# Strassen's seven products for the gated feed-forward projections of the second block

## The chip, the cores and the metric

The kernel runs on one core of one Trainium2 chip. The metric is the device time in microseconds (us). Before the change the median of three runs is 2394.31 us (2393.95 to 2394.52). A difference of under 0.2% (some 5 us) can hardly be told from none.

## The reference, cut to what matters

The program takes 512 tokens of width 1024 through two blocks of two layers each, in float32. The change touches the feed-forward part of the second block's two layers, which the reference computes as

```python
D_FF_2 = 2816
def swiglu(h, w_gate, w_up, w_down):
    return (jax.nn.silu(h @ w_gate) * (h @ w_up)) @ w_down
x = x + rmsnorm(swiglu(rmsnorm(x, ffn_pre_g[layer]), ...), ffn_post_g[layer])
```

with `w_gate` and `w_up` of 1024 x 2816 and `w_down` of 2816 x 1024. The first block has an ungated part of this kind: relu(h w_up) squared, times w_down.

## The kernel before, in words

**Three passes.** Values are kept with features on the 128 partitions and the 512 tokens in the free dimension. Every float32 operand is split into a high and a low fp32r part, and a product is three matmuls: high by high, high by low, low by high. The weights are split on the chip. SyncE loads a slot (a 512 x 512 or smaller piece of a weight matrix) into one of three raw buffers (`load_slots`, L317; a load waits until the low parts of the slot three before it are made), ScalarE copies it to the high part (`stream_hi` L341, `rows_hi` L329), GpSimd subtracts to get the low part (`stream_lo`, L397, operations on L414), and TensorE takes one 128 x 512 tile after the other as its low part is counted (`group_tiles`, matmuls on L452). Slots go through ScalarE and GpSimd strictly in the order in which they were planned.

**A group** is one filling of half of PSUM (four banks of 128 x 512). A direct projection group has 8 tiles of rows, 4 banks and 3 passes: 96 matmuls over 512 columns. A half of a down projection has 4 tiles of rows and 48 such matmuls. Groups alternate between the halves of PSUM, and a bank is taken again when VectorE has emptied it (`bank_free`).

**Strassen's seven products** are used before the change in the first block's feed-forward part (`quarter_tiles`, L488, matmuls on L485). The group's product is cut in two slots, each of seven units; a unit is one product of quarters: 4 tiles x 3 passes = 12 matmuls over 256 columns, so a group has 168. Four of a slot's seven weight units are sums of quarters of the raw weights, made by VectorE (`units_sum`, L380, operations on L395); the others are taken as loaded. ScalarE then makes the high part (`units_hi`, L377) and GpSimd the low one (L409). The low part is written over the sum, so GpSimd must wait for those later sums that still read it:

```python
pool.wait_ge(sems["sum_done"], slot.sum0 + (2, 4, 3, 4)[SUMS.index(k)])
```

with `SUMS = (1, 2, 3, 5)`. Unit 2 thus waits for all four sums. The weight units lie in eight cells used in turn; a cell comes free when TensorE has used its unit. Before TensorE's units 4, 5 and 6 the products of earlier units must be taken out of PSUM: a copy by ScalarE (`p1_copied`), then two adds (`p5_added`) and one more (`p7_added`) by VectorE (`middle`, L1936, rows on L1942 to L1946). For the moving side, four sums of quarters of h are made once per layer: ScalarE writes h in full precision (`hf`, L1704), VectorE subtracts (`t_total`, L1927), ScalarE makes the high parts (`t_high`, L1701) and VectorE the low ones.

**The second block's feed-forward part** before the change is direct. `plan_second` (L1212) plans 11 projection groups, each with 256 gate and 256 up features (2816 = 11 x 256), and the down projection in halves: first a short one for the first group's 256 rows, then four full ones of 512 rows and a last one that is joined to the norms (`Boundary`). Around them TensorE does projection groups 0 and 1, the short down projection, group 2, then down projection, group, group, and so on. `gated` (L2325, L2560) is the work after a group: VectorE takes four banks out with the norm's factor (L969, L978), ScalarE applies silu, VectorE multiplies (L2576), and the result is split (`hid_hi` L2333 by ScalarE, `hid_lo` L2579 by VectorE). `down` (L2582) adds a down projection's banks into `acc` (L2590). ScalarE's and VectorE's queues are written out by hand in `second_layer` (L2025): an instruction that waits holds up all behind it.

## Time and profile before

| | |
|---|---|
| runs | 2394.31 us median of 3 (2393.95 to 2394.52) |
| profiled execution | 2391.58 us, of which span 2389.8 us |
| TensorE busy | 2341.5 us (98%), 12840 matmuls |
| VectorE busy | 1347.5 us (56%) |
| ScalarE busy | 1047.3 us (44%) |
| GpSimd busy | 1229.2 us (51%) |
| DMA | 214.58 MB, mean 90 GB/s |

PE, DVE, ACT, POOL and SP are TensorE, VectorE, ScalarE, GpSimd and SyncE. In a timeline a row is a start, a duration, then the engine, line and operation; "x4" merges four in a row, and a bracket names the idle time before it and what ended it. The feed-forward parts of the second block run from about 1472 to 1812 us and from about 2008 to 2352 us of the span.

### The profile page before, as it was taken

The page shows a single profiled execution, that of the slowest core. Times are in us where ns is not written, and L with a number is a line of the kernel's source. Part 1 is how long each engine was busy: PE and PEld are TensorE (multiplying, and loading weights), DVE is VectorE, ACT ScalarE, POOL GpSimd, SP SyncE. Part 2 cuts the span into 40 slices and gives each one's busy share as a digit, 9 for nine tenths or more (in the row PEclk, how much of TensorE's full clock was granted, in tenths as well). Part 3 has the DMA queues.
Part 4 walks back from the last instruction along what each step waited for, and adds up shares of the span by engine and source line. Part 5 has one row for each costly group of instructions (what it writes and reads, how often), then busy time and mean ns, then how long its engine had stood idle before and what let it go on. Part 6 is the DMA issues. An engine that isn't in the chain of part 4 may idle for free.

```text
span 2389.8 us, 32547 instructions
## 1 busy us (share of the span) xinstructions
PE 2341.5 (98%) x12840; PEld 1929.5 (81%) x12840; DVE 1347.5 (56%) x2210; ACT 1047.3 (44%) x1654; POOL 1229.2 (51%) x915
## 2 busy tenths in 40 slices
PE   8999999999999999999999999999999999999997
PEld 6777688989877767898988769888889779888887
DVE  4687587675548866867665446322225768322224
ACT  5345573444343456553444455322224485322223
POOL 4435277786543253787783453554454334554442
PEclk9999999999999999999999999999999999999999
DMA  5213123232322131233232212322332312322331
GB/s 187 75 62 107 36 88 106 91 105 89 106 89 71 56 113 54 88 107 106 89 123 88 85 36 62 115 88 88 106 106 89 106 53 80 115 89 88 105 106 36
DMA packets 153975, 214.58 MB, mean 90 GB/s; under 512 B 7776, under 2 KB 94944, under 8 KB 153568
## 3 DMA queue, kind: packets, MB, share of 16 engines
q1 hardware_dynamic: 153824, 212.51, 27.3%
q8 instruction: 102, 1.67, 0.3%
q14 instruction: 49, 0.40, 0.1%
HBM read 208.30 MB, written 2.10 MB: 88 GB/s over the span
## 4 chain that ended last, share of the span: by engine, by line
PE 86%; DVE 5%; ACT 4%; POOL 3%; issue 2%; SPq 0%; DMA 0%; ACTq 0%; DVEq 0%; POOLq 0%
PE ps L452 64%; PE ps L485 13%; POOL w_lo L414 2%; PE ps L1024 2%; PE ps L1005 2%; PE ps L1047 1%; PE ps L2185 1%; PE ps L1499 1%; DVE h_lo L748 1%; DVE x L871 1%; DVE tmp_both L866 1%; PE ps L1537 1%; ACT w_hi L353 0%; PE ps L1546 0%; ACT L672 0%
## 5 line engine op out<-in xcount | busy, mean ns | idle before, releaser
L414 POOL TENSOR_TENSOR w_lo<-raw,w_hi 128x512 fp32r<-128x512 f32 (+1 forms) x648 | 859.6, 1365 | 982.4 <-ACT w_hi L353 977.1
L452 PE MATMUL ps<-h_hi,w_hi 128*128 128x512 f32 (+1 forms) x1248 | 507.4, 407 | 10.5 <-POOL w_lo L414 10.4
L452 PE MATMUL ps<-h_hi,w_lo 128*128 128x512 f32 (+1 forms) x1248 | 487.4, 391 | 0.0
L452 PE MATMUL ps<-h_lo,w_hi 128*128 128x512 f32 (+1 forms) x1248 | 487.2, 390 | 0.0
L452 PE MATMUL ps<-hid_hi,w_hi 128*128 128x512 f32 x928 | 366.9, 395 | 10.3 <-POOL w_lo L414 4.8
L452 PE MATMUL ps<-hid_hi,w_lo 128*128 128x512 f32 x928 | 361.5, 390 | 0.0
L452 PE MATMUL ps<-hid_lo,w_hi 128*128 128x512 f32 x928 | 361.4, 389 | 0.0
L353 ACT ACTIVATE w_hi<-raw 128x2048 fp32r<-128x2048 f32 (+2 forms) x145 | 246.3, 1724 | 172.9 <-PE ps L452 110.8
L452 PEld LDWEIGHTS ps<-h_hi,w_hi 128*128 128x128 f32 (+1 forms) x1248 | 234.5, 188 | 72.4 <-issue 18.0
L452 PEld LDWEIGHTS ps<-h_hi,w_lo 128*128 128x128 f32 (+1 forms) x1248 | 233.8, 187 | 51.5 <-issue 0.2
L452 PEld LDWEIGHTS ps<-h_lo,w_hi 128*128 128x128 f32 (+1 forms) x1248 | 234.3, 188 | 50.7 <-issue 5.5
L409 POOL TENSOR_TENSOR c_lo_more<-c_f_more,c_hi_more 128x512 fp32r<-128x512 f32 x112 | 171.7, 1548 | 120.7 <-DVE c_f_more L395 112.6
L452 PEld LDWEIGHTS ps<-hid_hi,w_hi 128*128 128x128 f32 x928 | 174.4, 188 | 52.9 <-POOL w_lo L414 8.3
L452 PEld LDWEIGHTS ps<-hid_hi,w_lo 128*128 128x128 f32 x928 | 174.2, 188 | 36.7
L452 PEld LDWEIGHTS ps<-hid_lo,w_hi 128*128 128x128 f32 x928 | 174.3, 188 | 35.1 <-issue 1.0
L377 ACT ACTIVATE c_hi_more<-c_f_more 128x512 fp32r<-128x512 f32 x112 | 70.5, 631 | 240.5 <-DVE c_f_more L395 238.9
L969 DVE TENSOR_TENSOR tmp_both<-ps,rstd 128x512 f32<-128x512 f32 x48 | 33.0, 690 | 248.2 <-PE ps L452 248.1
L2330 ACT ACTIVATE tmp_both<-tmp_both 128x512 f32<-128x512 f32 x44 | 27.6, 631 | 267.7 <-DVE tmp_both L969 266.4
L1865 DVE TENSOR_TENSOR x<-x,ps 128x512 f32<-128x512 f32 x160 | 102.3, 679 | 75.3 <-PE ps L452 75.3
L1130 ACT ACTIVATE p<-p,stat 128x128 f32<-128x128 f32 (+3 forms) x128 | 71.8, 561 | 136.8 <-DVE stat L1092 136.6
L485 PE MATMUL ps<-t_hi,c_lo_more 128*128 128x256 f32 x448 | 126.5, 282 | 0.0
L485 PE MATMUL ps<-t_lo,c_hi_more 128*128 128x256 f32 x448 | 126.3, 282 | 0.0
(355 smaller groups left out, 4524.6 us busy)
## 6 DMA issues: line engine op xcount, KB each, us to landing
raw<-in_w_down SPq DMA_DIRECT2D x32, 1024.0 KB, 4.9
raw_u<-in_w_up SPq DMA_DIRECT2D x28, 1024.0 KB, 5.2
raw<-in_ffn_w_gate SPq DMA_DIRECT2D x44, 512.0 KB, 3.8
raw<-in_ffn_w_up SPq DMA_DIRECT2D x44, 512.0 KB, 4.7
raw<-in_w_in SPq DMA_DIRECT2D x20, 1024.0 KB, 5.0
raw<-in_ffn_w_down SPq DMA_DIRECT2D x20, 1024.0 KB, 4.9
raw<-in_w_out SPq DMA_DIRECT2D x8, 1024.0 KB, 6.4
raw<-in_ev_w_in SPq DMA_DIRECT2D x8, 1024.0 KB, 5.1
```

The costliest lines, as they stand in the source:

```text
L353: act.activation(w_hi[slot.buf][:, k:k + n, 0:slot.width], raw[r][:, k:k + n, 0:slot.width], ACT.Copy).then_inc(sems["hi_split"], n)
L377: act.activation(unit(slot.hi(i)), of, ACT.Copy).then_inc(sems["hi_split"], 1)
L409: pool.tensor_tensor(unit(slot.lo(k)), of, unit(slot.hi(k)).bitcast(F32), ALU.subtract).then_inc(sems["lo_split"], 1)
L414: pool.tensor_tensor(slot.lo(k)[:, 0:slot.width], raw[r][:, k, 0:slot.width], slot.hi(k)[:, 0:slot.width].bitcast(F32), ALU.subtract).then ...
L452: mm = pe.matmul(o, lh, rh, start=first and q == 0, stop=last and q == 2, skip_group_check=True)
L485: mm = pe.matmul(o, lh, rh, start=first and q == 0, stop=last and q == 2, skip_group_check=True)
L969: sg["bank_free"].by(dve.tensor_tensor(o, src, rstd[:, 0:width], ALU.mult))
L1005: mm = pe.matmul(ps[:, e, 0:n], a_q[rows, j, q], a_k[rows, kb, 0:n], start=c == 0, stop=last)
L1024: mm = pe.transpose(ps[:, 2, kb * P:(kb + 1) * P], p_t[i % self.PB][:, kb * P:(kb + 1) * P], ident)
L1130: sg["p_ready"].by(act.activation(p_t[i % self.PB][:, 0:w], p_t[i % self.PB][:, 0:w], ACT.Exp, bias=sn[:, i:i + 1], scale=SCALE, accum_out ...
L1865: sg["bank_free"].by(dve.tensor_tensor(x[:, b, :], x[:, b, :], ps[:, HALF * st.groups[g].half + m, :], ALU.add))
L2330: sg["relu_ready"].by(act.activation(tmp[m][:], tmp[m][:], ACT.Silu))
```

## The change

Of the 11 projection groups of each second-block layer, nine (numbers 2 to 10) are computed by seven products; each slot then holds 128 gate and 128 up columns side by side, loaded by two transfers. Seven cells take the place of eight here: a unit always gets the cell of the same unit of the slot before. The order on TensorE is now group 0, group 1, the two halves of the short down projection, group 2, group 3, and then one half of a down projection ahead of each of the groups 4 to 10, the last half, and the joined one. ScalarE makes `hf` and VectorE `t_total` ahead of `gated` for group 0. VectorE's order in one group is `strassen`; the banks of the down half that TensorE did before the group are added behind the group's first joins, ahead of the last two weight sums. The diff, cut:

```diff
@@ -188,6 +188,16 @@
...
+        ffn_cells = [("gap", 0), ("more", 0), ("more", 1), ("more", 7), ("tab", 0), ("h", 0), ("h", 1)]
@@ -293,10 +303,11 @@
...
+                    self.need[s % RING] += 16 * len(src)
...
+                    pieces = [(w.rearrange("(k p) c -> p k c", p=P), 256 // len(src) * n, 256 // len(src))
+                              for n, w in enumerate(src)]
+                    slot = Slot(pieces, UNITS, self.need[s % RING], None, self.rows)
@@ -1235,19 +1248,24 @@
...
+            def gated_quarters(c0, half):
+                return st.quarters([[w[:, c0 + P * i:c0 + P * i + P] for w in (wg, wu)] for i in range(2)], half)
+
+            def down(r0, rows, n, half):
+                return st.group(cols(wd, [(512 * n, 512)], r0), [rows], half)
 
             pl.s_ffn = len(st.slots)
-            pl.up, pl.down = [up(CH2 * 512, first)], []
-            for c in range(CH2):
-                if 0 < c < CH2 - 1:
-                    pl.down.append(down(512 * (c - 1), KT, 1 - first))
-                pl.up.append(up(512 * c, 1 - first))
-                if c == 0:
-                    pl.down.append(down(CH2 * 512, REST2 // P, first))
-                pl.up.append(up(512 * c + 256, first))
-            pl.down.append(down(512 * (CH2 - 2), KT, 1 - first))
+            pl.up, pl.down = [up(CH2 * 512, first), up(0, 1 - first)], []
+            pl.down.append([down(CH2 * 512, REST2 // P, n, (first + n) % 2) for n in range(2)])
+            pl.up.append(gated_quarters(256, first))
+            pl.up.append(gated_quarters(512, 1 - first))
+            for n in range(4, UPS):
+                c, e = divmod(n - 4, 2)
+                if e == 0:
+                    pl.down.append([])
+                pl.down[-1].append(down(512 * c, KT, e, first))
+                pl.up.append(gated_quarters(256 * (n - 1), 1 - first))
+            pl.down[-1].append(down(512 * (CH2 - 2), KT, 1, first))
@@ -1300,11 +1318,23 @@
...
+                turn, downs = 0, 0
+                for i in range(pl.s_ffn, pl.s_out + 2):
+                    slot, n = st.slots[i], i - pl.s_ffn
+                    if slot.quarters:
+                        slot.cells = [ffn_cells[(turn + k) % len(ffn_cells)] for k in range(slot.rows)]
+                        turn += slot.rows
+                        slot.buf = None
+                    elif n < 4:
+                        slot.buf = (4, 3, turns[0], turns[1])[n]
+                    elif n < 6:
+                        slot.cells, slot.buf = [(turns[0], 2 * (n - 4) + k) for k in range(2)], None
+                    elif i >= pl.s_out:
+                        slot.buf = 2 + i - pl.s_out
+                    else:
+                        slot.buf = turns[1 - downs % 2]
@@ -2195,19 +2237,21 @@
...
+                for e in range(2):
+                    rest(tiles_of(pl.down[0][e], FEAT, hid_hi, hid_lo, ready=("hid_lo_done", lo0)))
+                quarter_tiles(pe, pl.up[2], 0, "t_done", t_hi2, t_lo2)
+                quarter_tiles(pe, pl.up[3], 2, None, t_hi2, t_lo2)
+
+                def down(c, e):
+                    pe.wait_ge(*at("hid_lo_done", 4 * c + 6))
+                    rest(tiles_of(pl.down[1 + c][e], FEAT, hid_hi, hid_lo, k0=KT * (1 - c % 2)))
+
+                for n in range(4, UPS):
+                    down(*divmod(n - 4, 2))
+                    quarter_tiles(pe, pl.up[n], 2 * (n - 2), None, t_hi2, t_lo2)
+                down(CH2 - 2, 1)
+                pe.wait_ge(*at("hid_lo_done", 2 * UPS))
+                to_next.tensor(pe, 2, None, KT)
@@ -2332,14 +2376,55 @@
...
+                for k in range(DB):
+                    sg["hf_done"].by(act.activation(hf[k // 4][:, k % 4, :], x[:, k, :], ACT.Copy, scale=pl.pre_ffn.gain(k)))
+                gated(pl.up[0], 0)
+                for n in range(4):
+                    t_high(n)
+                stream_hi(act, s_ffn + 6)
+                units_hi(act, u_slot(2), 0, 5)
+                gated(pl.up[1], KT)
+                units_hi(act, u_slot(2), 5, 7)
+                for n in range(2, UPS):
+                    nx = u_slot(n + 1) if n + 1 < UPS else None
+                    ub = u_slot(n) + 1
+                    units_hi(act, ub, 0, 1)
+                    p1_copy(n, 0)
+                    units_hi(act, ub, 1, 7)
+                    if n >= 3:
+                        stream_hi(act, ub + 2)
+                    p1_copy(n, 1)
+                    if nx is not None:
+                        units_hi(act, nx, 0, 5)
+                    silu(n, 0)
+                    if nx is not None:
+                        units_hi(act, nx, 5, 6)
+                    silu(n, 1)
+                    if nx is not None:
+                        units_hi(act, nx, 6, 7)
+                    hid_high(n, 1)
+                    hid_high(n, 0)
+                stream_hi(act, s_out + 2)
                 if even:
@@ -2589,17 +2674,87 @@
...
+                def join(n, i):
+                    t, u = slice(256 * i, 256 * i + 256), 2 * (n - 2) + i
+                    dve.wait_ge(*at("p1_copied", u + 1))
+                    dve.wait_ge(sems["unit_used"], st.slots[u_slot(n) + i].unit0 + 3)
+                    link(dve, dve.tensor_tensor(u_p16[:, i, :], u_p1[:, i, :], bank(n, 3)[:, t], ALU.add))
+                    sg["p5_added"].by(dve.tensor_tensor(u_q[0][:, i, :], u_p16[:, i, :], bank(n, 1)[:, t], ALU.add))
+                    dve.wait_ge(*at("p5_added", u + 1))
+
+                def join_more(n, i):
+                    t = slice(256 * i, 256 * i + 256)
+                    dve.wait_ge(sems["unit_used"], st.slots[u_slot(n) + i].unit0 + 4)
+                    sg["p7_added"].by(dve.tensor_tensor(u_q[0][:, i, :], u_q[0][:, i, :], bank(n, 2)[:, t], ALU.add))
+
+                def strassen(n):
+                    ub, nx = u_slot(n) + 1, u_slot(n + 1) if n + 1 < UPS else None
+                    units_sum(dve, ub, 0, 1)
+                    join(n, 0)
+                    units_sum(dve, ub, 1, 2)
+                    join_more(n, 0)
+                    if n >= 4:
+                        down(1 + (n - 4) // 2, n % 2)
+                    units_sum(dve, ub, 2, 4)
+                    join(n, 1)
+                    if nx is not None:
+                        units_sum(dve, nx, 0, 1)
+                    join_more(n, 1)
+                    dve.wait_ge(*at("p7_added", 2 * (n - 1)))
+                    link(dve, dve.tensor_tensor(u_q[0], u_q[0], both(rstd, 1), ALU.mult))
+                    if nx is not None:
+                        units_sum(dve, nx, 1, 2)
+                    dve.wait_ge(sems["unit_used"], st.slots[ub].unit0 + 5)
+                    ins = dve.tensor_tensor(u_q[1], two(bank(n, 0)), both(rstd, 0), ALU.mult)
+                    sg["bank_free"].by(ins)
+                    if nx is not None:
+                        units_sum(dve, nx, 2, 3)
+                    dve.wait_ge(sems["unit_used"], st.slots[ub].unit0 + 6)
+                    sg["bank_free"].by(dve.tensor_tensor(u_q[2], u_p16, two(bank(n, 1)), ALU.add))
+                    dve.wait_ge(sems["bank_free"], BANKS + HALF * pl.up[n] + 2)
+                    sg["gate_ready"].by(dve.tensor_tensor(u_q[2], u_q[2], both(rstd, 1), ALU.mult))
+                    if nx is not None:
+                        units_sum(dve, nx, 3, 4)
+                    dve.wait_ge(sems["bank_ready"], HALF * (pl.up[n] + 1))
+                    sg["bank_free"].by(dve.tensor_tensor(u_q[3], u_p16, two(bank(n, 2)), ALU.add), 2)
+                    dve.wait_ge(sems["bank_free"], BANKS + HALF * pl.up[n] + 4)
+                    link(dve, dve.tensor_tensor(u_q[3], u_q[3], both(rstd, 0), ALU.mult))
+                    dve.wait_ge(*at("relu_ready", 2 * n + 2))
+                    sg["v_ready"].by(dve.tensor_tensor(u_q[2], u_q[2], u_q[0], ALU.mult))
+                    sg["v_ready"].by(dve.tensor_tensor(u_q[3], u_q[3], u_q[1], ALU.mult))
+                    for e in (1, 0):
+                        dve.wait_ge(*at("hid_hi_done", 2 * n + 2 - e))
+                        sg["hid_lo_done"].by(dve.tensor_tensor(hid_quad(hid_lo, n, e), u_q[3 - e],
+                                                               hid_quad(hid_hi, n, e).bitcast(F32), ALU.subtract))
+
+                dve.wait_ge(*at("hf_done", DB))
+                for n in range(4):
+                    t_total(n)
+                gated(pl.up[0], 0)
+                for n in range(4):
+                    t_low(n)
+                units_sum(dve, u_slot(2), 0, 3)
+                gated(pl.up[1], KT)
+                units_sum(dve, u_slot(2), 3, 4)
+                down(0, 0)
+                down(0, 1)
+                for n in range(2, UPS):
+                    strassen(n)
+                down(CH2 - 1, 1)
                 to_next.vector(dve)
```

## Rows read from the trace of the kernel before

**Rows 1.** TensorE's busy time and granted clock, the page's parts 1 and 2:

```profile
PE 2341.5 (98%) x12840; PEld 1929.5 (81%) x12840; DVE 1347.5 (56%) x2210; ACT 1047.3 (44%) x1654; POOL 1229.2 (51%) x915
...
PEclk9999999999999999999999999999999999999999
```

**Rows 2.** The chain of waits, the page's part 4, shares by engine:

```profile
PE 86%; DVE 5%; ACT 4%; POOL 3%; issue 2%; SPq 0%; DMA 0%; ACTq 0%; DVEq 0%; POOLq 0%
```

**Rows 3.** Windows: stretch, its length, each engine's busy time, clock, DMA share, GB/s:

```profile
414.50:434.50 20.00, 20.00 (x169) 19.99 (x168) 9.30 (x15) 10.85 (x20) 13.06 (x11) 1.00 0.21 71
434.50:456.30 21.80, 21.80 (x98) 18.05 (x97) 19.89 (x18) 7.17 (x13) 19.50 (x12) 1.00 0.39 129
1554.40:1576.20 21.80, 21.80 (x98) 18.06 (x97) 8.07 (x12) 8.56 (x6) 17.10 (x14) 1.00 0.34 102
```

**Rows 4.** TensorE's timeline: the run's start, then first matmuls of groups:

```profile
8.78 0.63 PE L452 MATMUL ps<-h_hi,w_lo 128*128 128x512 f32 x1
...
10.92 0.49 PE L452 MATMUL ps<-h_lo,w_hi 128*128 128x512 f32 x1
...
414.50 0.29 PE L485 MATMUL ps<-h_hi,c_hi_more 128*128 128x256 f32 x1
...
434.52 0.40 PE L452 MATMUL ps<-hid_hi,w_hi 128*128 128x512 f32 x1
...
456.30 0.29 PE L485 MATMUL ps<-h_hi,c_hi_more 128*128 128x256 f32 x1
...
1521.16 0.39 PE L452 MATMUL ps<-hid_hi,w_hi 128*128 128x512 f32 x1
```

**Rows 5.** TensorE's timeline, the first block's first down projection:

```profile
349.94 0.50 PE L452 MATMUL ps<-hid_hi,w_hi 128*128 128x512 f32 x1 [0.71 <-POOL w_lo L414]
...
352.88 0.50 PE L452 MATMUL ps<-hid_hi,w_hi 128*128 128x512 f32 x1 [0.73 <-POOL w_lo L414]
```

**Rows 6.** VectorE's timeline in the first block's Strassen stage:

```profile
443.47 3.48 DVE L1971 TENSOR_TENSOR hid_lo<-tmp_both,hid_hi 128x512 fp32r<-128x512 f32 x2
...
450.27 4.26 DVE L1865 TENSOR_TENSOR x<-x,ps 128x512 f32<-128x512 f32 x7
...
458.02 0.69 DVE L395 TENSOR_TENSOR c_f_more<-raw_u 128x512 f32<-128x512 f32 x1 [0.83 <-PE ps L485]
...
462.00 0.41 DVE L1942 TENSOR_TENSOR rs<-p_more,ps 128x256 f32<-128x256 f32 x1
...
463.71 0.69 DVE L395 TENSOR_TENSOR c_f_more<-raw_u,c_f_more 128x512 f32<-128x512 f32 x1 [0.40 <-PE ps L485]
```

**Rows 7.** GpSimd's timeline in the same stage:

```profile
442.95 5.15 POOL L409 TENSOR_TENSOR c_lo_more<-c_f_more,c_hi_more 128x512 fp32r<-128x512 f32 x3
...
451.47 2.53 POOL L409 TENSOR_TENSOR c_lo_more<-raw_u,c_hi_more 128x512 fp32r<-128x512 f32 x2
...
464.55 2.54 POOL L409 TENSOR_TENSOR c_lo_more<-c_f_more,c_hi_more 128x512 fp32r<-128x512 f32 x2 [3.02 <-DVE c_f_more L395]
...
470.78 10.62 POOL L414 TENSOR_TENSOR w_lo<-raw,w_hi 128x512 fp32r<-128x512 f32 x7
```

**Rows 8.** VectorE's timeline, start of the first block's Strassen stage:

```profile
312.80 1.23 DVE L1927 TENSOR_TENSOR t_sum<-hf 128x1024 f32<-128x1024 f32 x1 [2.44 <-ACT hf L1704]
```

**Rows 9.** ScalarE's timeline, the same start:

```profile
307.76 5.00 ACT L1704 ACTIVATE hf<-x,vec 128x512 f32<-128x512 f32 x8
...
321.00 1.06 ACT L1701 ACTIVATE t_hi<-t_sum 128x1024 fp32r<-128x1024 f32 x1 [1.18 <-DVE t_sum L1927]
```

**Rows 10.** VectorE's timeline, start of the second block's feed-forward part:

```profile
1506.65 0.69 DVE L978 TENSOR_TENSOR tmp_both<-ps,rstd 128x512 f32<-128x512 f32 x1 [11.38 <-ACT rstd L693]
...
1510.69 1.30 DVE L2579 TENSOR_TENSOR hid_lo<-sq_both,hid_hi 128x512 fp32r<-128x512 f32 x2
```

**Rows 11.** ScalarE's timeline, the same start:

```profile
1510.03 1.24 ACT L2333 ACTIVATE hid_hi<-sq_both 128x512 fp32r<-128x512 f32 x2 [0.30 <-DVE sq_both L2576]
```

**Rows 12.** Issues of Strassen slots: KB each, us to landing:

```profile
raw_u<-in_w_up SPq DMA_DIRECT2D x28, 1024.0 KB, 5.2
```

More of the change, by code:

```diff
@@ L1194, in plan_first @@
                 if c < CH1:
[L1195 removed]
+                    pl.up.append(st.quarters([[a["w_up"][L][:, 512 * c + 256 * i:512 * c + 256 * i + 256]] for i in range(2)], half))
                     half = 1 - half
@@ L2602, in _, with t_total, t_low @@
-                down(CH2 - 1)
+                def t_total(n):
+                    b11, b12, b21, b22 = (hf[i][:, :, tokens(e)] for i in range(2) for e in range(2))
+                    p, q = ((b12, b11), (b22, t_sum2[:, 0]), (b22, b12), (b21, t_sum2[:, 1]))[n]
+                    if n in (1, 3):
+                        dve.wait_ge(*at("t_summed", (n + 1) // 2))
+                    sg["t_summed"].by(dve.tensor_tensor(t_sum2[:, n], p, q, ALU.subtract))
+                def t_low(n):
+                    dve.wait_ge(*at("t_high", n + 1))
+                    sg["t_done"].by(dve.tensor_tensor(t_lo2[:, n], t_sum2[:, n], t_hi2[:, n].bitcast(F32), ALU.subtract))
@@ new lines, in bank @@
+                def bank(n, b):
+                    return ps[:, HALF * st.groups[pl.up[n]].half + b, :]
+                def join(n, i):
[5 more added lines that the diff above has]
+                    dve.wait_ge(*at("p5_added", u + 1))
```

93 lines of the change are left out of this document (45 added, 48 removed).

## The prediction

> **What bounds the kernel now.** I read the page first: TensorE is busy 98% of the span at full granted clock [rows 1], and the chain of waits is 86% TensorE's [rows 2]. Then the windows: in the second block's stage TensorE is busy all of a 21.8 us stretch, while VectorE has 8.07 and GpSimd 17.10 us of work at its fullest (the last of [rows 3]). So time falls only if TensorE's work falls and the helpers keep up. Last, the timelines of the first block, which already does there what the change brings here: they give a price for almost every new step.
>
> **TensorE's part.** A Strassen group lasts from 414.50 to 434.52, 20.02 us; the 96 matmuls over 512 columns behind it last to 456.30, 21.78 us [rows 4]. A direct group has the same 96. So a changed group saves 1.76 us, and nine in each of two layers 31.7 us. That is all there is to win.
>
> Here the row is weighed against a rule. Over 256 columns a matmul takes 20.02/168 = 119 ns, over 512 columns 21.78/96 = 227 ns: more than half. The Trainium skill ("TensorE: Matmul & The Clock Gate", section Back-to-back issue gap) gives N/2.4 + 2.5 ns for an isolated gap, which as an estimate is 109 and 216 ns, 2.4 us a group and 43 us in all; the same section warns that it counts no weight loads. The trace disagrees.
>
> **What the helpers pay.** Alone, a GpSimd low part of 128x512 takes 2.54/2 = 1.27 us, say 1.26 with the 2.53 row; a VectorE operation on PSUM 4.26/7 = 0.61. But a VectorE operation with two SBUF inputs next to a GpSimd one slows both: VectorE 3.48/2 = 1.74, GpSimd 5.15/3 = 1.72 [rows 6, 7]. So each such operation pushes GpSimd back by 1.72 - 1.26 = 0.46 us. PSUM adds do not (the seven run at 0.61 while GpSimd works). The Trainium skill ("SBUF — State Buffer", Who interferes with whom) calls it an exclusive lock for the full instruction; that would be 1.26 + 0.61 = 1.87 a pair, and 0.8 us more stall per down half than below, 12 us in all. The row's 1.72 decides.
>
> **The steady cycle**, a Strassen group and half a down projection, seven times a layer. Clock t from TensorE's first matmul; a unit is 20.02/14 = 1.43 us; a wait on a unit ends 0.29 late (the sum at 458.02 for the unit done at 457.73) [rows 6]. VectorE has one more wait here than in the first block, since with seven cells slot 1's unit k must wait for slot 0's unit k, not k-1.
> - First join: third unit, 4.29 + 0.29, then two of 0.45: 5.5. Weight sum 0.65: 6.1. Third add 0.45: 6.6.
> - Four adds of the down half at 0.61: 9.0. Before, they lay beside idle time; here the last two weight sums stand behind them.
> - Two weight sums: 10.3. In the first block the last sum starts at 463.71 - 456.30 = 7.4, and GpSimd goes on at 464.55, 8.25 [rows 6, 7]. Here at 10.4, because unit 2 waits for all four sums.
> - GpSimd then has five units and the four tiles of the next down half, 9 x 1.26 = 11.3. Beside them VectorE asks for five two-input operations (first sum of the next slot, the up factor, second and third sum, the gate factor): 2.3. Last tile ready at 24.0.
> - TensorE wants that tile at 20.02 + 3 x 0.68 = 22.06. It stalls 1.95 us. The first block shows this form: tile after tile of its first down projection waits for GpSimd, 0.71 and 0.73 us [rows 5]; in its steady stage GpSimd starts those tiles at 470.78, t = 14.5 [rows 7], and none waits.
> So the cycle is 20.02 + 10.89 + 1.95 = 32.86 us, against 21.78 + 10.89 = 32.67 now. The gain of 1.76 is spent and 0.2 more. VectorE's tail (two products, two low parts, all beside GpSimd) ends about 0.5 us before it is needed for the next group. The banks are free at t = 25, long before TensorE is back at 33.
>
> **The start of a layer.** Now evacuation of group 0 starts at 1506.65, and its high and low parts end at 1511.27 and 1511.99 [rows 10, 11]. New ahead of it: ScalarE's eight `hf`, 5.0 us, and VectorE's four `t_total` at some 1.2, 4.75 us [rows 8, 9]. Both ends move by 9.75, to 1521.0 and 1521.7; TensorE asks at 1521.16 [rows 4], so the hidden values are just in time. The short down projection's weights are not: ScalarE splits them behind group 0's high parts and four `t_high` of 1.0 (1.06 [rows 9]): 1524.9, first tile 0.5, GpSimd 1.26: 1526.7. Stall 5.5 us.
> - Group 2: VectorE takes group 1 through `gated` (5.3, as group 0 now [rows 10]), the fourth weight sum, eight bank copies (4.9) and a sum before its first join, done about 1545.9; TensorE needs it 7.15 us after 1537.6. It is 1.1 late and the third add 0.3 more. Stall 1.4.
> - Group 3 follows group 2 with no down projection between. VectorE's fourth sum for it ends some 3.8 us after the group begins (0.9 if nothing met GpSimd, 7 if all did; I went through both queues). Then six two-input operations at 1.72, since GpSimd has five units to do as well, and the join 0.9: 15.0. TensorE needs it at 7.15. Stall 7.9.
> - The first full down half stalls 1.1, the other seven 1.95. At the end the joined projection's weights are split behind the last group's: 0.5.
>
> **At nothing:** the transfers. They are two of 512 KB for one of 1 MB; one of 1 MB lands in 5.2 us [rows 12], and every slot has 9 us or more from its raw buffer's release to its first use. ScalarE has idle time: 10.85 us of work in a 20 us group [rows 3]. The longest stall, near 8 us, might cost TensorE's pace: at the run's start matmuls come 0.43 us apart instead of 0.23 for 3.1 us [rows 4]. Between 0 and 1.5 us each; I take 0.
>
> **Sum.** A layer: 5.5 + 1.4 + 7.9 + 1.1 + 7 x 1.95 + 0.5 = 30.0 of stalls, less 15.8 gained: +14.2. Two layers: +28.4. The profiled execution took 2391.58 (span 2389.8 and 1.8 around it), so 2420.0; the runs' median lies 2.7 above it: 2422.7, I say 2422.
>
> **Rivals.**
> 1. *The helpers keep pace, faster.* Place: the unit 2 low part at t = 10.4. If it starts by 8.45, the down half's tiles are ready and the steady stall is nil. For it: the first block gets to 8.25. Against it: four adds and the seventh cell lie before it. Startup would then cost some 11 a layer: 2394.3 - 31.7 + 22 = 2385; with that hidden too, 2363.
> 2. *It comes out even.* Steady stalls nil, the start as priced (15.3 a layer): 2394.3 - 31.7 + 30.6 = 2393.
> 3. *VectorE becomes the bound.* If all 15 two-input operations of a cycle meet GpSimd, VectorE has 25.8 + 7.2 (adds and joins on PSUM) = 33.0 us, more than the cycle, and each first join is late as in group 3. For it: in the first block's down stretch VectorE is busy 19.89 of 21.80 us [rows 3]. Against: GpSimd is idle from about t = 4 to 10. From 1.5 us a cycle: 2422 + 14 x 1.5 = 2443.
> 4. *The place of the adds does nothing.* Behind the last sums they would free GpSimd at 9.5 (unit 5's cell is free only at 8.9). The stall would still be about 1: this moves 14 us, not the sign.
>
> **How the numbers follow.** Forecast 0.60 (its own range 2406 to 2438), rival 3 0.12, rival 2 0.10, rival 1 0.18. The range takes in the upper half of rival 1 and most of rival 3: 2382 to 2442. Under 0.2% (4.8 us) a measurement of this kernel can't tell from no change. Faster: rival 1 and a third of rival 2, 0.21; same: 0.08; slower: 0.71.
>
> **What would show it.** Strassen groups of the second block at 20.0 us where nothing waits; waits of L452's `hid` matmuls on GpSimd's low parts of 1 to 2 us in each down half; a gap of 5 to 6 us ahead of the short down projection; in group 3 a gap of 5 us or more that VectorE's join ends; GpSimd idle in each group until t = 10, ended by a VectorE weight sum; GpSimd's mean low part above 1.4 us. I am wrong if TensorE's idle time per layer in this stage is under 16 us, above all if the down halves run through.

## The result, and the profile after

The changed kernel takes 2418.99 us (median of 4 runs, 2416.49 to 2424.13), the kernel before 2394.13 us beside it (4 runs, 2392.93 to 2394.52): ratio 1.0107, 95% interval 1.0089 to 1.0125, slower. The profiled execution is the run of 2416.49 us, with a span of 2414.7 against 2389.8. It is the fastest of the four; every stretch below is read from the one profiled execution of its kernel, every time and ratio from all runs.

The page's parts 1 and 4 of the changed kernel:

```profile
PE 2329.3 (96%) x14136; PEld 1969.8 (82%) x14136; DVE 1685.6 (70%) x2514; ACT 1152.8 (48%) x1934; POOL 1449.0 (60%) x1023
...
PE 68%; DVE 12%; POOL 10%; ACT 5%; issue 4%; SPq 0%; DMA 0%; DVEq 0%; ACTq 0%; POOLq 0%
```

TensorE is busy 12 us less than in [rows 1] (matmuls at half pace, told of below, count as busy) and the chain leaves it for VectorE and GpSimd, 22% together where [rows 2] has 8. The windows give the first full steady cycle in three parts, a Strassen group, a down half and the next group (busy time of PE, PEld, DVE, ACT and POOL, then clock, DMA share and GB/s):

```profile
1601.40:1621.40 20.00, 20.00 (x169) 20.00 (x168) 13.92 (x19) 7.58 (x12) 15.17 (x12) 1.00 0.29 85
1621.40:1633.80 12.40, 11.58 (x51) 8.93 (x51) 12.30 (x12) 5.25 (x9) 12.40 (x8) 1.00 0.36 120
1633.80:1653.80 20.00, 20.00 (x169) 20.00 (x168) 13.92 (x19) 7.58 (x12) 15.17 (x12) 1.00 0.29 86
```

The group runs without a gap; the down half lasts 12.3 us instead of 10.9, and VectorE and GpSimd are busy throughout. Below, layer 0 and layer 1 are the two layers of the second block. The gaps in TensorE's work, its timeline in layer 0 from the last matmul of the direct groups on (in brackets the idle time and what ended it):

```profile
1521.31 0.39 PE L464 MATMUL ps<-h_hi,w_lo 128*128 128x512 f32 x1
1528.13 0.77 PE L464 MATMUL ps<-hid_hi,w_hi 128*128 128x512 f32 x1 [6.43 <-issue]
1528.70 0.63 PE L464 MATMUL ps<-hid_lo,w_hi 128*128 128x512 f32 x1
...
1533.79 0.39 PE L464 MATMUL ps<-hid_lo,w_hi 128*128 128x512 f32 x1
...
1566.08 0.39 PE L497 MATMUL ps<-t_hi,c_hi_more 128*128 128x256 f32 x1 [1.21 <-POOL c_lo_more L421]
...
1571.56 0.36 PE L497 MATMUL ps<-h_hi,c_hi_tab 128*128 128x256 f32 x1 [2.09 <-ACT p_more L2385]
...
1575.93 0.36 PE L497 MATMUL ps<-h_hi 128*128 128x256 f32 x1 [2.72 <-DVE tmp_both L2696]
...
1657.20 0.50 PE L464 MATMUL ps<-hid_hi,w_hi 128*128 128x512 f32 x1 [0.72 <-POOL w_lo L426]
```

The first pair is the gap ahead of the short down projection, 6.6 us beyond the usual spacing; behind it matmuls start 0.43 us apart for 5.3 us before they are back at 0.23. The next three lie in group 3, which follows group 2 with nothing between. The last is the fourth low part of a down half, and its like stands in every cycle. What ended the first gap, which TensorE's row calls "issue", ScalarE's and GpSimd's timelines show:

```profile
1524.99 2.17 ACT L349 ACTIVATE w_hi<-raw 128x512 fp32r<-128x512 f32 x4
```

```profile
1525.68 7.44 POOL L426 TENSOR_TENSOR w_lo<-raw,w_hi 128x512 fp32r<-128x512 f32 x4 [16.43 <-ACT w_hi L349]
```

GpSimd stood idle until ScalarE rounded the short down projection's weights.

**Where the time went, by stretch.** All matmuls of a direct group and a down half cost 21.78 and 10.89 us; a changed group measures 20.07. In layer 0, from the direct groups' end to the first full down half (1521.54 to 1588.92) are 67.4 us, of which 10.88 + 2 x 20.07 = 51.0 are work: **16.4 us of stall at the start** (16.5 in layer 1). The eight down halves last 12.46, six between 12.28 and 12.36, and 11.53: **10.8 us of stall in the halves**. From layer 0's joined projection to the next layer's work (its first matmul on L677) are 31.14 us against 29.65 before: 1.5 at the **boundary** between the two layers. Nine groups give back 9 x 1.71 = 15.4. From the end of the direct groups to the joined projection a layer is 305.8 us against 294.3, 11.5 more in either layer (16.4 + 10.8 - 15.4 = 11.8; the kernel before had some 0.3 of waits in this stretch too); twice that, 1.5 and 0.4 ahead of it are the 24.9 us of the two spans.

### The profile page after: what moved, and what is told of

Read it like the earlier page. It is cut to its first block, busy times and chain, and to the rows that moved or that the text cites. A ratio compares the mean times of both kernels' runs of the same rounds, so it can differ in the third digit from the quotient of the medians.

```text
span 2414.7 us, 36406 instructions
## 1 busy us (share of the span) xinstructions
PE 2329.3 (96%) x14136; PEld 1969.8 (82%) x14136; DVE 1685.6 (70%) x2514; ACT 1152.8 (48%) x1934; POOL 1449.0 (60%) x1023
## 4 chain that ended last, share of the span: by engine, by line
PE 68%; DVE 12%; POOL 10%; ACT 5%; issue 4%; SPq 0%; DMA 0%; DVEq 0%; ACTq 0%; POOLq 0%
PE ps L464 43%; PE ps L497 15%; POOL w_lo L426 5%; DVE c_f_more L407 2%; PE ps L1036 2%; PE ps L1017 2%; DVE acc L2675 1%; PE ps L1059 1%; POOL c_lo_more L421 1%; POOL h_lo L421 1%; POOL c_lo_tab L421 1%; POOL h_hi L421 1%; PE ps L2227 1%; PE ps L1533 1%; DVE h_lo L760 1%
## 5 line engine op out<-in xcount | busy, mean ns | idle before, releaser
L426 POOL TENSOR_TENSOR w_lo<-raw,w_hi 128x512 fp32r<-128x512 f32 (+2 forms) x504 | 712.7, 1447 | 699.4 <-ACT w_hi L365 661.2
L421 POOL TENSOR_TENSOR c_lo_more<-c_f_more,c_hi_more 128x512 fp32r<-128x512 f32 x220 | 329.3, 1513 | 216.5 <-DVE c_f_more L407 153.2
L464 PE MATMUL ps<-hid_hi,w_hi 128*128 128x512 f32 x928 | 373.1, 402 | 35.0 <-POOL w_lo L426 15.4
L464 PE MATMUL ps<-h_hi,w_hi 128*128 128x512 f32 (+1 forms) x672 | 283.3, 422 | 11.1 <-POOL w_lo L426 11.1
L464 PE MATMUL ps<-h_hi,w_lo 128*128 128x512 f32 (+1 forms) x672 | 263.3, 392 | 0.0
L464 PE MATMUL ps<-h_lo,w_hi 128*128 128x512 f32 (+1 forms) x672 | 263.1, 391 | 0.0
L497 PE MATMUL ps<-t_hi,c_hi_more 128*128 128x256 f32 x880 | 248.3, 282 | 2.4 <-POOL c_lo_more L421 2.4
L407 DVE TENSOR_TENSOR c_f_more<-raw_u 128x512 f32<-128x512 f32 x128 | 170.4, 1331 | 41.7 <-PE ps L497 41.2
L497 PEld LDWEIGHTS ps<-t_hi,c_hi_more 128*128 128x128 f32 x880 | 165.8, 188 | 3.3 <-POOL c_lo_more L421 3.3
L497 PEld LDWEIGHTS ps<-t_lo,c_hi_more 128*128 128x128 f32 x880 | 165.9, 188 | 0.0
L497 PEld LDWEIGHTS ps<-t_hi,c_lo_more 128*128 128x128 f32 x880 | 165.6, 188 | 0.0
```

The source lines that it names most:

```text
L407: sg["sum_done"].by(dve.tensor_tensor(o, p, q, op))
L421: pool.tensor_tensor(unit(slot.lo(k)), of, unit(slot.hi(k)).bitcast(F32), ALU.subtract).then_inc(sems["lo_split"], 1)
L426: pool.tensor_tensor(slot.lo(k)[:, 0:slot.width], raw[r][:, k, 0:slot.width], slot.hi(k)[:, 0:slot.width].bitcast(F32), ALU.subtract).then ...
L464: mm = pe.matmul(o, lh, rh, start=first and q == 0, stop=last and q == 2, skip_group_check=True)
L497: mm = pe.matmul(o, lh, rh, start=first and q == 0, stop=last and q == 2, skip_group_check=True)
```

## The experiments

All change the changed kernel and leave its arithmetic alone; only orders and places move. My theory was the prediction's: low parts come late because of where steps stand in the engines' queues. Its rival was that VectorE and GpSimd lack time as such. The expectations of all twelve stand in full, those that failed too. Ratios are to the kernel before. Executions differ by some us ahead of the stage (the short down projection was asked for between 1521.5 and 1526.3), so stretches are compared by their own length.

### e1: the adds behind the last sums

```
                     units_sum(dve, ub, 1, 2)
                     join_more(n, 0)
-                    if n >= 4:
-                        down(1 + (n - 4) // 2, n % 2)
                     units_sum(dve, ub, 2, 4)
+                    if n >= 4:
+                        down(1 + (n - 4) // 2, n % 2)
```

> The changed kernel with VectorE's four down adds behind the second weight slot's last two sums instead of ahead of them. If the stall of 1.44 us in a down half comes from GpSimd waiting for these sums until 10.25 us after the group's start: GpSimd goes on some 0.9 us earlier, in each of the 14 halves with adds the stall falls by 0.8 to 1.0, 2405 to 2409 us. If the place of the adds does not matter (the rival in which the stall is GpSimd's amount of work or the shared time of its operations with VectorE's): within 2 us of 2419.

2413.22 us, ratio 1.0072 (1.0054 to 1.0090). That is outside the expected 2405 to 2409. A steady down half lasts 11.7 to 11.75, a stall of 0.8 instead of 1.44: GpSimd goes on 9.64 us after the group's start instead of 10.25, and now the fourth sum itself waits 0.66 us for TensorE to free its cell. The last half has no stall, the first none in layer 0 and 1.6 as before in layer 1. So the halves give 5.8 and 4.1 us. The starts take 16.9 and 15.8 instead of 16.4 and 16.5, and the boundary, reached earlier, 36.0 instead of 31.1: 9.9 + 0.1 - 4.9 = 5.1, and 5.8 came of it in the time. So the place of the adds counts, and something at the boundary takes half of it back. GpSimd's row for unit 2 in the group that begins at 1635.39, then VectorE's and GpSimd's timelines at the boundary, show both:

```profile
1645.03 2.55 POOL L421 TENSOR_TENSOR c_lo_more<-c_f_more,c_hi_more 128x512 fp32r<-128x512 f32 x2 [2.04 <-DVE h_f L407]
```

```profile
1836.20 5.08 DVE L656 TENSOR_TENSOR ssum<-ssum,sq_both 128x512 f32<-128x512 f32 x1
```

```profile
1825.64 15.10 POOL L426 TENSOR_TENSOR w_lo<-raw,w_hi 128x512 fp32r<-128x512 f32 x12
```

One sum of squares took 5.08 us. It ends 0.5 us after GpSimd's run of low parts (1840.74), which was at its undisturbed pace (15.10/12 = 1.26). More of this below.

### e2, e5, e8: the start's queues

e2 moves `stream_hi(act, s_ffn + 6)`, the short down projection's weights, ahead of ScalarE's `gated(pl.up[0], 0)`.

> ScalarE rounds the short down projection's weights right behind its eight copies of the normed block, ahead of the first gated columns. If ScalarE's queue makes the 6.6 us gap at the layer's start: the gap falls below 1.5 us, the 2.8 us of slow pace behind it go with it, and groups two and three give some of it back because their weights' parts are made no earlier: 4 to 9 us less per layer, 2401 to 2411. If the gap is the wait for the hidden values or for the transfers: within 2 us of 2419, with the gap ending on another releaser.

2421.56 us, ratio 1.0113 (1.0098 to 1.0128): nothing gained. TensorE's timeline in layer 0 has two gaps in place of one:

```profile
1527.27 0.50 PE L464 MATMUL ps<-hid_hi,w_hi 128*128 128x512 f32 x1 [2.92 <-DVE hid_lo L2664]
1536.52 0.77 PE L464 MATMUL ps<-hid_hi,w_hi 128*128 128x512 f32 x1 [3.53 <-DVE tmp_both L981]
```

The first ends on the hidden values, the second on the bank that VectorE empties when it comes to group 1. ScalarE's queue was the last releaser of the gap, not its only cause. In layer 1 the second gap is shorter and the start takes 14.8 us instead of 16.5; the boundary, 35.9 us instead of 31.1, spends that and more. e5 put VectorE in order too, and moved ScalarE's `hf` and `t_high` behind the columns they had stood ahead of. VectorE's part:

```
-                dve.wait_ge(*at("hf_done", DB))
-                for n in range(4):
-                    t_total(n)
                 gated(pl.up[0], 0)
+                dve.wait_ge(*at("hf_done", DB))
                 for n in range(4):
-                    t_low(n)
-                units_sum(dve, u_slot(2), 0, 3)
+                    t_total(n)
                 gated(pl.up[1], KT)
-                units_sum(dve, u_slot(2), 3, 4)
+                for n in range(4):
+                    t_low(n)
+                units_sum(dve, u_slot(2), 0, 4)
```

> Both engines take the first gated columns ahead of everything for the Strassen groups: ScalarE gated columns, short down's weights, the eight block copies, second gated columns, four roundings; VectorE gated columns, four block differences, second gated columns, four low parts, four weight sums. With ScalarE's order alone mended (the run before) the 6.8 us gap only split into 3.3 us for the hidden values and 3.9 us for the bank that VectorE empties late. If the gap is both engines' order: no gap ahead of or in the short down projection and no slow pace, 9.4 us per layer gained, of which group two's wait for its low parts takes 2 to 5 back: 2404 to 2412. If it is VectorE's total of work up to group three: the gaps move into groups two and three whole, within 3 us of 2419.

2420.43 us, ratio 1.0114 (1.0097 to 1.0131). The gap ahead of the short down projection is gone, and stands at full size ahead of group 2:

```profile
1539.18 0.55 PE L497 MATMUL ps<-h_hi,c_hi_gap 128*128 128x256 f32 x1 [6.31 <-DVE acc L2672]
```

e8 filled 6 us of VectorE's and ScalarE's idle time ahead of group 1's columns with three weight sums and four roundings, and emptied each bank when it was wanted, the short projection's second half behind group 2's first joins. VectorE's part, as it differs from e5:

```
                 gated(pl.up[0], 0)
+                units_sum(dve, u_slot(2), 0, 3)
...
                 gated(pl.up[1], KT)
+                down(0, 0)
                 for n in range(4):
                     t_low(n)
-                units_sum(dve, u_slot(2), 0, 4)
-                down(0, 0)
-                down(0, 1)
+                units_sum(dve, u_slot(2), 3, 4)
```

> The mended order of the start, and with it work put where the engines stood idle: VectorE's first three weight sums and ScalarE's first four roundings of group two go into the 6 us ahead of the second gated columns, VectorE empties the short down projection's first half ahead of the four low parts, its second half behind group two's first joins. The last start run turned the gap into one of 6.7 us ahead of group two that ended on VectorE's copy out of the bank: if it is that queue, it goes, and groups two and three keep their 6 to 7 us: 9 to 10 us per layer below the changed kernel, 2399 to 2405. If the amount of VectorE's work decides, 2412 or more.

2418.91 us, ratio 1.0097 (1.0077 to 1.0118): no gain. But here the gaps did shrink, in layer 0 from 13.1 to 9.8 us, 4.0 in group 2 and the rest in group 3. In layer 0 TensorE's pace took it back, and the start stalls 17.3 us; in layer 1 the start takes 14.8 instead of 16.5, and the boundary 35.9 instead of 31.1. Two windows of e8, behind the first gap and among the last ones:

```profile
1540.80:1550.00 9.20, 9.20 (x54) 9.20 (x55) 6.02 (x10) 1.57 (x4) 7.86 (x6) 0.66 0.34 100
...
1570.00:1580.00 10.00, 7.65 (x35) 7.41 (x36) 8.19 (x9) 3.45 (x7) 6.04 (x5) 0.55 0.36 105
```

The granted clock is 0.66 and 0.55 where the changed kernel, with much the same three gaps in group 3, has 1.00 in layer 0 and 0.83 in layer 1, where the clock fell behind the second gap:

```profile
1570.00:1580.00 10.00, 5.72 (x46) 5.58 (x47) 9.04 (x9) 4.08 (x8) 6.50 (x5) 1.00 0.37 107
...
2119.00:2129.00 10.00, 6.55 (x42) 6.31 (x43) 9.45 (x10) 3.67 (x7) 6.50 (x5) 0.83 0.36 106
```

Beside the gaps e8 loses 7.5 of its 17.3 us in layer 0, some 6 of them to matmuls at half pace, the changed kernel 3.3 of its 16.4, and 4.5 of its 16.5 in layer 1 with the same orders. So the pace is not set by the orders alone. TensorE's row of the first, and GpSimd's of e9, which has the same start:

```profile
1540.81 0.58 PE L497 MATMUL ps<-t_hi,c_hi_more 128*128 128x256 f32 x1 [3.97 <-POOL c_lo_more L421]
```

```profile
1543.04 2.83 POOL L435 TENSOR_TENSOR c_lo_more<-c_f_more,c_hi_more 128x512 fp32r<-128x512 f32 x2 [15.01 <-DVE h_f L421]
```

GpSimd stood idle for 15 us. Unit 2's low part overwrites the second sum, which the fourth still reads, and I had left the fourth behind the low parts of the block sums: my own order, not the amount of work.

### e3, e4: slots ahead, and a down half between

e3 takes each full down half's weights one group earlier through SyncE's loads, ScalarE's rounding and GpSimd's low parts, TensorE's order unchanged:

```
+            for n in range(3, UPS):
+                c, e = divmod(n - 3, 2)
+                s = st.slot_ahead(cols(wd, [(512 * e, 512)], 512 * c), KT, 1)
+                pl.up.append(gated_quarters(256 * (n - 1), 1 - first))
...
+                pl.down[-1].append(st.group_of(s, first))
```

> Each full down half's weights are loaded, rounded and split one Strassen group earlier, ahead of that group's own weights; TensorE's order is as it was. If the down half waits for low parts that are just late in GpSimd's order: the 1.44 us go in all 14 steady halves and the 1.57 of the first, about 21 us, and group three starts with four tiles more ahead of it, up to 5 us per layer lost: 2398 to 2409. If GpSimd is short of time as such, each group's first tiles wait instead and the time is within 3 us of 2419.

2406.79 us, ratio 1.0049 (1.0034 to 1.0064). Two windows of the trace, a group and its down half:

```profile
1606.40:1626.40 20.00, 20.00 (x169) 20.00 (x168) 14.51 (x19) 7.59 (x12) 14.48 (x12) 1.00 0.29 86
1626.40:1637.30 10.90, 10.90 (x50) 9.04 (x49) 10.80 (x11) 4.82 (x9) 10.90 (x7) 1.00 0.40 134
```

No down half waits: cycles of 30.98 us against 32.67 before. So in the steady stage the rival falls: the helpers do a cycle's work in less than TensorE needs. The rest of the sum: halves -21.2, start 19.9 and 19.1 instead of 16.4 and 16.5 (four more low parts ahead of group 3, a gap of 4.2 us there), boundary 34.3 instead of 31.1: -21.2 + 6.1 + 3.2 = -11.9, measured -12.2.

e4 ran the short down projection's second half between groups 2 and 3.

> The second half of the short down projection runs between Strassen groups two and three instead of ahead of group two. If group three's 7.0 us of stall are the join of group two and group three's weights with nothing between them: up to 5.4 us of other matmuls lie there now, group two starts 5.4 us earlier and waits part of that for its own weights; 2 to 5 us less per layer, 2409 to 2415. If it is GpSimd's and VectorE's total of work at the start: within 2 us of 2419.

2419.42 us, ratio 1.0104 (1.0089 to 1.0119), as the rival had it; start 16.8 and 15.5. In layer 0 group 3 stalled 5.6 instead of 7.0 and group 2, begun earlier, 2.7 instead of nothing. The stall moved once more; in layer 1 it lost 1.0 on the way.

### e6, e7, e9, e10: combinations

e6 joins e5's start and e3's earlier slots, all but the first down half's; e7 adds ScalarE's `p1_copy(n + 1, 0)` ahead of `hid_high(n, ...)` for group 3.

> The order of the run above, and every down half's weights but the first one group earlier. If the two losses are apart: another 1.44 us in each of 14 halves, less 2 to 3 us that VectorE's block sums at the end of each layer take back (as where all halves were ahead): 14 to 16 below the run above, 2389 to 2397. If a third place binds instead, 2400 or more.

> As the run above, and in ScalarE's order the copy of each Strassen group's first product stands ahead of the rounding of the group before's hidden values. If the 2.37 us wait in group three is that copy's place: 0 to 2.4 us less per layer (the join of VectorE comes 3 us later and may bind anyway), 0 to 5 us below the run above. If only VectorE's join binds: no change within 1 us.

2413.61 and 2412.88 us, ratios 1.0090 (1.0075 to 1.0105) and 1.0084 (1.0069 to 1.0099). e6 is far above the 2389 to 2397 that was expected; e7 is 0.7 below e6, which is what was expected if only VectorE's join binds. All but the first half run through, and the start takes 21.9 and 22.6 us in e6, 21.1 and 23.1 in e7. ScalarE rounds two down slots in one go in group 3, and the copy that the join needs waits behind the second's transfer (a gap of 4.8 us in e6, ended by the join). e7's copy changed the releaser of group 3's wait and not its end.

e9 is e8's start, e6's slots with that second slot behind the copy, e7's copy, and group 2's `hid_low` behind group 3's first joins. e10 adds e4's split.

> The start of the run above; every down half's weights but the first one group earlier, with the second such slot's rounding behind the copy of group three's second first product (it delayed that copy by 5.1 us before); and for group two alone the hidden values' low parts behind group three's first joins, with ScalarE's copy ahead of its two roundings. If all of these are queue order: 14 halves times 1.44 less 5 at the layers' ends, and 3 to 5 us of group three's wait per layer: 22 us or so below the run above, 2377 to 2387, under the kernel before. If GpSimd and VectorE lack time as such: 2390 or more.

> As the run above, with the short down projection's second half between groups two and three. Group three's join gets 5.4 us, group two starts 5.4 us earlier, when its low parts are made only some 4 us later: between 3 us per layer better and 3 us worse than the run above, 2374 to 2390; if group three's wait is gone and group two waits instead by as much, the two runs are even.

2407.15 and 2411.81 us, ratios 1.0059 (1.0040 to 1.0077) and 1.0073 (1.0058 to 1.0089); start 19.5 and 21.1 in e9, 21.7 and 22.0 in e10. Both missed by 20 us and more, e9 on the side of its rival; e10 is 4.7 us slower than e9, where 6 either way was expected. In e9 the waits are GpSimd's 15 idle us again and, in group 3, VectorE's timeline:

```profile
1592.28 1.32 DVE L421 TENSOR_TENSOR c_f_more<-raw_u 128x512 f32<-128x512 f32 x1 [7.12 <-DMA raw_u<-in_ffn_w_up]
1593.52 0.41 DVE L2726 TENSOR_TENSOR tmp_both<-tmp_both,ps 128x256 f32<-128x256 f32 x1
```

A weight sum for group 4 waits 7.12 us for its transfer, which could start only once GpSimd had left the raw buffer, three slots back; the third add of group 3 (L2726) is queued behind it, and TensorE behind that.

### e11 and e12: the fourth sum, and no double run

e11 is e9 with VectorE's `units_sum(dve, u_slot(2), 3, 4)` moved ahead of `gated(pl.up[1], KT)`, one more of ScalarE's roundings ahead of group 1's columns and the last two between its `t_high`, and group 3's `join_more(n, 1)` ahead of the sum that waited.

> The orders of e9 with two places mended that its trace showed. VectorE's fourth weight sum of group two, for which GpSimd's low part of the second stood still 15 us, goes ahead of the second gated columns (ScalarE's roundings five to seven with it); and in group three the sum for the next group, which waited 7 us for its transfer with the last join behind it, goes behind that join. If the start is order after all: of the 19.5 us of stall per layer between the first gated columns and the first full down projection, 4 in group two and 5 to 6 in group three go: 2384 to 2392, at or under the kernel before. If what is left is bound by the work of VectorE and GpSimd or by the seven cells that group three's parts share with group two: less than 4 us per layer goes, 2400 or more.

2406.15 us, ratio 1.0047 (1.0033 to 1.0060). Up to the first full down half the stall is 10.8 us (11.0 in layer 1), the least of all runs; then group 4 takes 27.6 instead of 20.1 (29.0 in layer 1). VectorE's and GpSimd's timelines:

```profile
1588.60 6.52 DVE L421 TENSOR_TENSOR c_f_more<-raw_u 128x512 f32<-128x512 f32 x1 [6.56 <-DMA raw_u<-in_ffn_w_up]
```

```profile
1583.29 10.03 POOL L440 TENSOR_TENSOR w_lo<-raw,w_hi 128x512 fp32r<-128x512 f32 x8
```

An operation that takes 0.69 us alone took 6.52, until GpSimd was through its run of eight (1593.32) and one more low part (1594.57); in layer 1 its like took 6.69. e12 keeps the start, drops the double run by having all halves ahead as in e3, and leaves out e11's last move.

> The start of e11 and group three's order, with all down halves' weights one group earlier as in e3, so that GpSimd never has two such slots in one run. In e11 what groups two and three gained (61.9 us from the short down projection's start to the first full one, against 70.5 in e9) was lost in group four: a weight sum of VectorE took 6.5 us beside GpSimd's run of eight low parts. If that sum was held by that run: no operation of VectorE over 4 us there and group four 20.1 us, against some 5 us more in group three, whose parts come four tiles later; 2396 to 2404. If group four's loss has another cause, such as the transfer it waited for: it stays near 7 us, 2408 or more. If VectorE's and GpSimd's work at the start bounds all orders: stall of 16 to 20 us from the short down projection's start to the second full one, wherever it lies, and 2404 to 2408.

2394.95 us (11 runs) against 2393.96 (15 runs): ratio 1.0003, 0.9994 to 1.0012, no difference from the kernel before, and 24 us under the changed one. Group 4 takes 20.07 and no operation there is held. It is a little better than expected (2396 to 2404). The sum closes: halves -21.2; start 14.0 and 14.4 instead of 16.4 and 16.5, -4.5; boundary 32.8 instead of 31.1, +1.7: -24.0. The largest gap left in the start, ahead of group 3, is ended by GpSimd:

```profile
1565.97 0.58 PE L511 MATMUL ps<-h_hi,c_hi_gap 128*128 128x256 f32 x1 [6.36 <-POOL c_lo_gap L435]
```

**What the runs settle, and what they don't.** The start of each layer in each trace, the stall in us from the direct groups' end to the first full down half, and what of it is gaps (over 0.9 us from one matmul's start to the next, less the usual spacing) and what is slower pace and small waits; last the boundary between the layers:

```
             after   e1    e2    e3    e4    e5    e6    e7    e8    e9   e10   e11   e12
layer 0
  stall       16.4  16.9  18.1  19.9  16.8  18.6  21.9  21.1  17.3  19.5  21.7  10.8  14.0
  gaps        13.1  13.1  12.4  13.7  11.3  12.1  17.9  16.1   9.8  13.7  16.1   6.2  10.3
  the rest     3.3   3.8   5.7   6.2   5.5   6.5   4.0   5.0   7.5   5.8   5.6   4.6   3.7
layer 1
  stall       16.5  15.8  14.8  19.1  15.5  17.5  22.6  23.1  14.8  21.1  22.0  11.0  14.4
  gaps        12.0  13.0  11.1  13.2  11.1  12.4  18.0  17.5   9.8  16.1  16.9   7.8   9.2
  the rest     4.5   2.8   3.7   5.9   4.4   5.1   4.6   5.6   5.0   5.0   5.1   3.2   5.2
boundary      31.1  36.0  35.9  34.3  31.2  33.5  32.8  34.4  35.9  32.8  32.8  34.2  32.8
```

The steady stall is an order and goes whole (e3). The start's is not one queue's. Where one wait was cleared (e2, e5, e4) the next came out on another engine, and the 1 to 1.7 us that layer 1 of e2 and e4 kept did not come out in the time. Only what also used idle time (e8, e11, e12) brought the gaps under 11 us in both layers; e11 paid its 10.8 with 8.3 more right behind. The times of e4, e5, e8 and e9 came out where their expectations had the rival, the engines' work; against it, e12 took 4.5 us off the two starts by orders alone. The pace is a second lever, and partly chance: e1 has the same three gaps in group 3 in both layers, and the lower clock behind them only in layer 0, so 1 to 3 us per layer of these sums are not the orders' doing. Whether an order would go well under 10 us of gaps and keep it, or this is what the block sums (the sums of quarters of h) and seven cells cost where two Strassen groups follow each other, stays open. Two starts of 14 and the 3 us at the boundary are the 31 us that the products save.

## Why the prediction was right, step by step

Forecast 2422 (profiled execution 2420.0), measured 2418.99 (2416.49); slower, as given 0.71. The mechanism was right in the main; that the time came so close is in part luck, for the terms were off by more than their sum.

- **TensorE's part.** 20.07 us per group for the 20.02 of [rows 4]; 9 x 1.71 for 9 x 1.76. Right, and the direct matmuls kept their 227 ns.
- **The steady cycle.** Right in mechanism, a little long. VectorE's timeline, and below it GpSimd's, for the group that begins at 1633.78:

```profile
1636.90 1.54 DVE L407 TENSOR_TENSOR c_f_more<-raw_u 128x512 f32<-128x512 f32 x1 [1.40 <-PE ps L497]
...
1640.20 2.48 DVE L2675 TENSOR_TENSOR acc<-acc,ps 128x512 f32<-128x512 f32 x4
1642.60 0.68 DVE L407 TENSOR_TENSOR c_f_more<-raw_u 128x512 f32<-128x512 f32 x1
1643.20 0.69 DVE L407 TENSOR_TENSOR h_f<-raw_u,c_f_more 128x512 f32<-128x512 f32 x1
```

```profile
1644.03 2.55 POOL L421 TENSOR_TENSOR c_lo_more<-c_f_more,c_hi_more 128x512 fp32r<-128x512 f32 x2 [2.62 <-ACT c_hi_more L389]
...
1650.30 6.85 POOL L426 TENSOR_TENSOR w_lo<-raw,w_hi 128x512 fp32r<-128x512 f32 x4
```

  The adds end at 8.9 (forecast 9.0), the sums at 10.1 (10.3), unit 2 starts at 10.25 (10.4), the last tile is there at 23.4 (24.0). That the fourth sum holds unit 2 fits its end, 1643.89, though the bracket names ScalarE's rounding of the third, 1644.00; in e1, where the two lie apart, GpSimd's row names the fourth sum. The four down tiles meet VectorE one and all, 1.71 each as the rows of 1.72 had it; the five units before them meet it not at all. Four meetings, where I counted five: 0.46 less, and the stall is 1.44 for 1.95. The first half stalls 1.6 for 1.1, and the last 0.6, which I had taken like the others. Over a layer the halves cost 10.8 for 1.1 + 13.65 = 14.75.
- **The start.** The gap: 5.5 forecast, 6.6 measured. The path was as told, ScalarE's rounding behind `hf`, group 0 and `t_high`; GpSimd's first low parts also met VectorE's `t_low`, 7.44/4 = 1.86 each instead of 1.26, which I had not counted. The slow pace behind it: taken 0, bounded by 1.5, measured 13.64 - 10.88 = 2.8. That bound failed; I had taken it from the run's start, 3.1 us at 0.43 apart [rows 4], and here it was 5.3 us. Group 2: 1.4 forecast, none: VectorE's first join ended 1.7 before TensorE asked, and TensorE was there 3.9 later than forecast by the gap and the slow pace. Group 3: 7.9 forecast, 7.0 measured. The stall ends with the join as said, 13.95 us after the group's start for 15.0; but it is three gaps, the first two ended by GpSimd and ScalarE, and the single one of 5 us or more that I had named as a sign is not there. In all I gave 14.8 for what measured 16.4. The terms hang together, though, which the sum did not say: e2, e5 and e4 each took one away and found most of it in the next.
- **The boundary.** Priced in the sum at 0.5 a layer for the joined projection's weights; between the layers it took 1.5, and up to 6.4 in the experiments (36.0 for 29.65).
- **Sum.** +14.2 per layer for 11.5 and the boundary once: 28.4 for 24.9. The errors were of both signs: per layer the halves 4.0 too high, the start 1.6 too low, and the boundary 0.5 too low over both layers.
- **Rivals.** 1, the helpers keep pace: not here, since unit 2 starts at 10.25 and not 8.45; e3 shows the premise sound, once the parts come earlier the stall is nil. 2, the steady stalls nil and the start as priced, 2393: not the changed kernel, but much what e12 came to (no stall in the halves, starts of 14.0 and 14.4 for 15.3, 2394.95). 4, the place of the adds: forecast a stall of about 1 and 14 us, measured 0.8 and 9.9 in the halves, but 5.8 in the time (e1). 3, VectorE as the bound: no steady group waits for its join, though VectorE is busy 12.30 of 12.40 us in a down half. It is as near as that.

## What to carry to other kernels

A step that makes the bound engine faster moves every deadline of its helpers forward, and this one gave them more work too: 31 us of matmul time were bought with 338 us more of VectorE's time and 220 of GpSimd's, [rows 1] against the page above. A wait's last releaser names the queue that came last, not the cause: mend both queues in the timeline, then count the stretch as a whole, since a stall that moves looks like one that is gone. And weights which one helper makes late should be asked for a whole stage earlier (e3), but not two such batches in a row on GpSimd where VectorE is due an operation with two SBUF inputs (e11).

## What the runs showed of the hardware that was not expected

**A VectorE operation can be held for a whole run of GpSimd's.** In the steady stage the two alternate, 1.74 and 1.71 us each. But a VectorE operation with two SBUF inputs that came while GpSimd was in an unbroken run of low parts took 4.44 to 5.21 us at the boundary in eleven of the twelve experiments, all but e4 (5.08 in e1, 4.45 in e3, 5.21 in e8, 4.44 in e12), and 6.52 and 6.69 in e11's two groups 4, each time until 0.5 to 0.6 us after GpSimd had ended its run, or one operation more, while GpSimd's kept 1.25 to 1.26. The Trainium skill ("SBUF — State Buffer", Who interferes with whom) says that a VectorE instruction with two SBUF inputs contends with a GpSimd one that reads SBUF, and calls the shared ports an exclusive lock. The rows agree with a block, but it lasted over three to five of GpSimd's instructions. It isn't always so: at the same place in the changed kernel's own trace, and in e4's, they alternate, and e9's weight sum for group 4, beside the same kind of run of eight as e11's, took 1.32 us. VectorE's rows of the changed kernel, then GpSimd's run in this window, 18.92/14 = 1.35 each:

```profile
1838.23 1.38 DVE L656 TENSOR_TENSOR ssum<-ssum,sq_both 128x512 f32<-128x512 f32 x1
...
1840.13 2.88 DVE L656 TENSOR_TENSOR ssum<-ssum,sq_both 128x512 f32<-128x512 f32 x2
```

```profile
1825.22 18.92 POOL L426 TENSOR_TENSOR w_lo<-raw,w_hi 128x512 fp32r<-128x512 f32 x14
```

What decides between the two was not tried. It is not how far GpSimd is into its operation when VectorE's comes: 0.43 us in e4, which alternates, 0.44 in e8, which holds. The two traces without a held operation have a boundary of 31.1 and 31.2 us and the eleven with one 32.8 to 36.0, so it is the likely cause of what the boundary took back, though no edit tried it by itself. Before the change GpSimd was idle there and the operation took 0.68 us.

**The pace after a gap.** In the window of the short down projection, behind the 6.6 us gap, TensorE's granted clock is 0.79, where the stages around it have 1.00:

```profile
1528.10:1541.80 13.70, 13.67 (x49) 11.07 (x50) 13.46 (x18) 5.84 (x10) 10.40 (x8) 0.79 0.53 155
```

The stretch at the lower level of 1.2 GHz (0.43 us a matmul for 0.23) was 5.3 us long, but 3.6 us behind the same gap in layer 0 of e1, and 3.8 us behind e12's gap of 6.5 us ahead of group 3. Shorter gaps in a row, 1.2 to 2.7 us each, brought it in layer 0 of e1 and e8 and not in layer 0 of the changed kernel, nor in layer 1 of e1. So its price could not be read from one place of the trace: half of 2 to 6 us for each time it falls.
